# One instruction instead of four for GpSimd's low parts of eight weight pieces in each second mixer

## The reference, cut to what matters

```
def hybrid_layer(x, mem, positions, ...):
    h = rms_norm(x, ln_mix)
    z = h @ w_in
    o_nsa = nsa_attention(...)
    o_gla = gated_linear_attention(...)      # the linear branch
    o_mem = memory_attention(...)
    gates = sigmoid(merge + b_merge)
    merged = (gates[:, :, 0] * (o_nsa @ w_branch[0])
              + gates[:, :, 1] * (o_gla @ w_branch[1])
              + gates[:, :, 2] * (o_mem @ w_branch[2]))
    x = x + merged @ w_out
    h = rms_norm(x, ln_mlp)
    return x + jnp.square(jax.nn.relu(h @ w_up)) @ w_down
```

## Time and profile before

| what | value |
|---|---|
| median of 3 runs | 1897.32 us |
| lowest, highest | 1897.01, 1897.33 us |
| span of the profiled execution, first to last instruction | 1895.7 us |
| median less that span | 1.6 us |
| PE busy | 1883.6 us (99%) |
| POOL busy | 1564.9 us (83%) |
| DVE busy, ACT busy | 1041.5 us (55%), 1042.5 us (55%) |
| instructions on POOL | 1139 |

### The profile page before, as it was taken

The page is one execution under the profiler, slowest core; times in us unless marked ns, Lnnn a source line. Parts: engine busy times, 40 slices in busy tenths (PEclk is TensorE's granted clock), DMA queues, the critical chain, the costliest instruction groups (busy, mean ns, idle before and its releaser), DMA issues.

```text
span 1895.7 us, 26703 instructions
## 1 busy us (share of the span) xinstructions
PE 1883.6 (99%) x9356; PEld 1540.3 (81%) x9356; DVE 1041.5 (55%) x2646; ACT 1042.5 (55%) x1777; POOL 1564.9 (83%) x1139
## 2 busy tenths in 40 slices
PE   9999999999999999999999999999999999999999
PEld 8888777888888878788888877788888877778887
DVE  5438465434676746553354677446443477645553
ACT  7445666444744476654466454655446554556543
POOL 8988876988798877698879787779887968788986
PEclk9999999999999999999999999999999999999999
DMA  7665434656575543367557343456757533346664
GB/s 288 236 234 189 153 130 150 195 192 197 203 238 190 196 159 132 118 225 260 191 186 260 123 145 116 152 178 209 241 194 259 168 129 128 125 153 196 193 192 142
DMA packets 98385, 348.97 MB, mean 184 GB/s; under 512 B 13228, under 2 KB 13900, under 8 KB 97740
## 3 DMA queue, kind: packets, MB, share of 16 engines
q1 hardware_dynamic: 97676, 346.13, 54.6%
q10 hardware_dynamic: 576, 1.14, 0.2%
HBM read 346.17 MB, written 1.05 MB: 183 GB/s over the span
## 4 chain that ended last, share of the span: by engine, by line
PE 91%; DVE 3%; ACT 3%; POOL 2%; issue 1%; POOLq 0%; ACTq 0%
PE psum L635 27%; PE psum L637 27%; PE psum L636 27%; POOL lo L608 2%; PE psum L704 1%; PE psum L887 1%; PE psum L877 1%; PE psum L900 1%; PE psum L1132 1%; PE psum L867 1%; ACT hi L1432 1%; DVE psum L2126 1%; ACT big L1835 0%; PE psum L1290 0%; PE psum L1083 0%
## 5 line engine op out<-in xcount | busy, mean ns | idle before, releaser
L608 POOL TENSOR_TENSOR lo<-raw,hi 128x256 fp32r<-128x256 f32 (+2 forms) x1129 | 1557.0, 1403 | 312.5 <-ACT hi L1432 283.3
L1432 ACT ACTIVATE hi<-raw 128x1024 fp32r<-128x1024 f32 (+1 forms) x613 | 639.5, 1053 | 491.7 <-PE psum L637 464.9
L635 PE MATMUL psum<-hi,h_hi 128*128 128x512 f32 (+1 forms) x1600 | 633.2, 396 | 1.9 <-DVE h_lo L2015 0.9
L637 PE MATMUL psum<-hi,h_lo 128*128 128x512 f32 (+1 forms) x1600 | 621.9, 389 | 0.0
L636 PE MATMUL psum<-lo,h_hi 128*128 128x512 f32 (+1 forms) x1600 | 621.3, 388 | 0.0
L635 PEld LDWEIGHTS psum<-hi,h_hi 128*128 128x128 f32 x1600 | 300.7, 188 | 69.8 <-issue 6.6
L2126 DVE STREAM_TRANSPOSE psum<-big 32x128 f32<-32x128 f32 (+1 forms) x960 | 344.0, 358 | 14.2
L637 PEld LDWEIGHTS psum<-hi,h_lo 128*128 128x128 f32 x1600 | 300.4, 188 | 62.5
L636 PEld LDWEIGHTS psum<-lo,h_hi 128*128 128x128 f32 x1600 | 300.9, 188 | 57.9
L635 PE MATMUL psum<-hi,y_hi 128*128 128x512 f32 x832 | 328.4, 395 | 0.4 <-DVE y_lo L2135 0.4
L637 PE MATMUL psum<-hi,y_lo 128*128 128x512 f32 x832 | 324.6, 390 | 0.0
(11 more groups left out here) (330 smaller groups left out, 1362.6 us busy)
## 6 DMA issues: line engine op xcount, KB each, us to landing
raw<-in_stream SPq DMA_DIRECT2D x607, 512.0 KB, 4.2
big<-in_w SPq DMA_DIRECT2D x14, 512.0 KB, 6.8
big<-in_post SPq DMA_DIRECT2D x6, 512.0 KB, 4.5
special<-in_b_merge SPq DMA_DIRECT2D x2, 1536.0 KB, 7.9
raw<-in_stream SPq DMA_DIRECT2D x8, 296.0 KB, 5.7
memkv<-in_mem_turned SPq DMA_DIRECT2D x2, 1024.0 KB, 6.3
big<-in_band SPq DMA_DIRECT2D x2, 768.0 KB, 4.9
raw<-in_first SPq DMA_DIRECT2D x2, 512.0 KB, 4.6
```

The source lines that it names most:

```text
L608: t = pool.tensor_tensor(M.lo[:, slot, w], M.raw[:, slot, w], f32(M.hi[:, slot_hi, w]), ALU.subtract)
L635: pe.matmul(out, lhs_hi, rhs_hi, start=start, stop=False)
L637: return pe.matmul(out, lhs_lo, rhs_hi, start=False, stop=stop)
L1432: act.activation(M.hi[:, slot_hi, used], M.raw[:, slot, used], ACT.Copy).then_inc(sem["hi"], 1)
```

## The change

Only the bound in `in_mixer` for the second kind of block changes (KD is 8):

```diff
@@ -581,7 +581,7 @@
     block, at = divmod(c, PIECES1) if c < L * PIECES1 else divmod(c - L * PIECES1, PIECES2)
     if c < L * PIECES1:
         return FFN_PIECES + 6 <= at < PIECES1 - FFN_PIECES - 4
-    return 12 <= at < PIECES2 - 8 * MLP_STRIPS - 4
+    return 12 <= at < PIECES2 - 8 * MLP_STRIPS - KD - 4
```

## The result

The changed kernel takes 1903.91 us (median of 5 runs, 1902.18 to 1905.13), the one before 1897.32 (5 runs, 1896.72 to 1897.63): a ratio of 1.0035, 95% interval 1.0024 to 1.0045. It is slower by 6.6 us, where +4.3 us was forecast, and lies above the range given.

The account below looks back on a forecast made before the run. PE, busy 99% of the span, was taken as the bound. L2426's delays of 2.16 and 2.15 us sum to 4.3 on the span of 1895.7, or 1901.6 us on the median of 1897.32; range 1896.9 to 1902.6.

Parts of the forecast that it names:

- Nothing to gain on POOL: Places 68 to 75, both second mixers: POOL's 11.2 us less work is covered by PE's own; gain taken as zero.
- The listed wait of PE: Whole kernel: PE's matmuls wait 0.8 us for POOL's low parts, in two places; this bounds the gain.
- Who comes first at the boundary: Start of place 68: POOL's whole piece begins 0.10 us ahead of DVE's L2426, which must wait; opposite order had chance 0.13.
- The size of that: L2426 after place 68: ends 1.08 us after the whole piece, so 2.16 and 2.15 us later in the two mixers.
- No slack, nothing absorbed: PE's transposes behind L2426: all its delay lands on PE, gap some 2.9 us; no later wait gives time back.
- PE's clock: Rival, PE's longer gap before the transposes: clock falls, 2.4 us more per mixer, +9.1 us, 1906.4; chance 0.05.
- The signs to look for: Both mixers: L2426 about 3.4 us, PE's wait about 5.8 us, POOL 6.8 us less busy, later stages unchanged.
- The remark that the transposes themselves would stand apart: PE's eight transposes after L2426: if they stand 0.2 us apart, the clock is the cause.

Follow-up runs that it names:

- taking it away in two ways: Against the changed kernel: place 68 cut in quarters again, 1896.95 us; or all eight places whole with POOL waiting for its own previous piece before place 68, 1896.63 us.
- the edit that leaves 1.9 us: The changed kernel plus 4 matmuls with unused result on PE before it waits for L2426: median 1902.68 us, ratio 1.0025 to the kernel before.
- the edit that leaves 1.06 us: The changed kernel plus 8 matmuls with unused result on PE before it waits for L2426: 1901.14 us, ratio 1.0020 to the kernel before.

## Why the prediction was right or wrong

- **Nothing to gain on POOL.** Read wrongly, and small. The listed wait of PE stayed, 0.8 and 0.9 us. But not all the low parts were there before PE came: place 75's came just in time to hold PE up, in both mixers. That term was put at zero and is 0.5 us in all, inside the 0.8 that was its bound.
- **Who comes first at the boundary.** Right, and shown by taking it away in two ways. Place 68 began 0.10 us ahead of L2426, as worked out from the earlier trace rows.
- **The size of that.** 2.16 and 2.15 us were forecast, 2.11 and 2.06 came; place 68 took 2.35 us where 2.40 was put in.
- **No slack, nothing absorbed.** Right but for the same place 75: with what stands around it 0.6 us came back.
- **PE's clock.** This is the step that failed. The gap was forecast right (2.9 us, measured 2.83 and 2.86), but that it lowers the clock got a chance of 0.05. I had argued that no row has PE idle that long. That is no evidence that the clock would hold, and in five of five runs of the change it fell, once at least. The price was put too high: 2.4 us a mixer, read off a stretch of 5.33 us at the start of the kernel; the slow ones here were 3.4 us long and cost 1.59 and 1.58. With the measured price the sum is 4.2 + 3.2 less the 0.6 given back and the 0.1 of a different start, 6.7 us. The two misses have opposite signs; without what came back the forecast would be further off. The Trainium skill's warning (TensorE: Matmul & The Clock Gate, section Why this matters for your kernels) was on the table and outweighed by a reading of absent rows. The trace agrees with it, and gaps shorter than those it warns of were enough: 2.8 us, 2.4, and 1.9 in five runs of eight.
- **The signs to look for.** L2426 at 3.4 us, the wait at 5.8 us, POOL 6.8 us less busy: measured 3.33, 5.7, 7.5. The remark that the transposes themselves would stand apart missed the place, since the clock fell only 1.1 and 0.5 us after PE had resumed, in the matmuls behind them. Not all later stages kept their lengths: place 66 took 1.6 us more.

## What to carry to other kernels

Where VectorE instructions with their inputs in SBUF run beside GpSimd's, each one that has to wait costs up to one GpSimd instruction, whatever its own size (up to 2.3 us for one of 0.17 here); long GpSimd instructions belong where no chain of small VectorE ones is awaited, or behind a semaphore that orders the two. A wait that looks superfluous (0.14 us of POOL waiting for itself) can be what lets the critical engine in first, so look at who is about to start before removing it. Look at the waits of the weight loads too: a wait for GpSimd stood there that the matmuls' own view didn't list. And when a change opens an idle gap of some 2 us or more on TensorE, add the price of a fallen clock to the sum; here the clock held through gaps of 1 us.

## What the runs showed of the hardware that was not expected

- The clock of TensorE fell to half, 1.2 GHz, after idle gaps of 5.1, 4.1, 2.8 and 2.4 us in every profiled execution that had them, and in five runs of eight with the edit that leaves 1.9 us; it was kept in 11 of 11 runs with the edit that leaves 1.06 us. The fall came up to 1.1 us after work had resumed, and cost 1.6 us each time in the changed kernel's profiled execution; a spell of twice the length cost 2.2 to 2.4 us. What decides at 1.9 us, no run here shows.
- It adds chance to an execution's time: the changed kernel's five runs spread over 2.95 us, the kernel before's over 0.91 us in five runs and 1.3 to 1.7 in 18 to 27.
- A VectorE instruction on 128 x 8 numbers takes 0.17 us alone, up to 0.67 us beside GpSimd's quarters, and 2.15 to 2.28 us beside its whole pieces.
